# Turning the expert rows on VectorE, from quarters written by ScalarE, in place of TensorE's transposes

## The chip, the cores and the metric

The kernel runs on one core of a Trainium2 chip. The metric is device time in microseconds of one execution, lower is better. TensorE (PE) multiplies and transposes into PSUM, VectorE (DVE) and ScalarE (ACT) do elementwise work, GpSimd (POOL) does some elementwise work and issues the indirect transfers, SyncE (SP) issues the plain ones.

## What is computed

A two-layer backbone over 256 latent tokens and 256 context tokens, width 1024. Each layer has a token mixer and then a mixture of 16 experts of which each token takes two. Layer 0 sends 512 tokens through its experts, layer 1 only the 256 latent ones. The part at stake:

```python
hid = jax.nn.silu(jnp.einsum('bld,edf->blef', h, w_gate)) * jnp.einsum('bld,edf->blef', h, w_up)
y = jnp.einsum('blef,efd->bld', hid * combine[..., None].astype(hid.dtype), w_down)
# D_MODEL = 1024, N_EXPERTS = 16, TOP_K = 2, D_EXPERT = 256, all float32
```

The reference multiplies every token by every expert; `combine` is zero but for the two that the router chose, and the kernel computes those alone.

## The kernel before

**Tiles.** After the router, each expert's tokens are gathered in tiles of 64 slots (`TILE`). With these inputs layer 0 has 24 tiles and layer 1 has 18, some of whose slots are empty. Each engine runs its own loop over the experts and, inside, over the expert's tiles; a tile's number over all experts is `q`.

**One tile, from row to output.** POOL gathers the tile's rows from DRAM into one of two buffers (`rows_in`, line 886): partitions 0 to 63 hold the first half of the width of the 64 slots, partitions 64 to 127 the second half. ACT copies them into `rows_flat` (line 789) in one instruction. PE turns them (`turn`, line 738): 8 transposes of 64x64 into PSUM. DVE copies the result into `slots_T` (line 827), whose eight slices of 64 columns are the stationary operands. PE multiplies gate and up (line 765): 8 slices of the width by 2 halves of the output columns, 16 multiplications, 32 in the trace, since a float32 one leaves two records. ACT takes silu of the gate half (line 800), DVE multiplies it by the up half (line 831), PE turns the product (line 776), DVE copies it out (line 836) and copies the expert's down weights into `down_now` (line 840; in layer 1 it multiplies them by the gate vector, line 843). PE multiplies by them (`down`, line 747), ACT copies the result from PSUM (`y_out`, line 795), and POOL scatters it to DRAM (line 914).

**The order on each engine is written by hand**, as a software pipeline. In its iteration for tile q, PE does gate and up of q, the turn of tile q+1, down of q-1, and the transpose of q's product. ACT does silu of q, the copy of the rows of q+2, and the output of q-1. DVE does the product of q, the copy of the turned rows of q+1, and the two copies for down of q. POOL copies two index columns (lines 903, 906), gathers and then scatters, always in this order, once per iteration; a gather into a buffer waits until ACT has copied the buffer's last rows (`rows_copied`).

**Weights.** SP loads gate, up and down weights of 1 MB each per expert, five experts deep (`sp_gate_up`, `sp_down`). A slot is loaded again when its expert's last gate and up multiplication, and then its last down copy, is done. Each partition k-slice holds rows `(j p k)` of the weights: two runs of 4 KB on a partition.

**Start of a layer.** The first tile's rows are copied, turned and copied out before the first gate and up multiplication can start.

## Time and profile before

| | us |
|---|---|
| Median of 3 runs (897.04 to 899.8) | 898.59 |
| The profiled execution | 899.06 |
| Its span, from first to last instruction | 897.2 |
| PE busy in the span | 762.4 |
| DVE busy | 493.1 |
| ACT busy | 315.3 |
| POOL busy | 308.5 |
| The experts of layer 0, first turn to last output copy | 131.4 to 291.7 |
| The experts of layer 1, the same | 750.6 to 874.7 |

The times of the last two rows are counted from the start of the span. A busy share is an average over stages with different limits; the expert stages are read on their own below. TensorE's clock was granted at 0.917 of full on average, and at full speed through nearly all of both expert stages.

### The profile page before, as it was taken

How to read it: one execution, taken by the hardware profiler on the slowest of the kernel's cores; microseconds unless marked ns; L12 is line 12 of the kernel's file. 1: busy time of each engine (PE TensorE's matmuls, PEld its weight loads, DVE VectorE, ACT ScalarE, POOL GpSimd, SP SyncE). 2: the span in 40 equal slices, each digit the busy share in tenths (PEclk: the TensorE clock that was granted, in tenths of full speed). 3: DMA queues.
4: the chain of work that ended last, by engine and by line, in shares of the span. 5: the costliest groups of instructions: out<-in, count | busy, mean ns of one | idle time of the engine just before them, and what ended most of it. 6: DMA issues, size and time to landing. Idle time of an engine off the chain costs nothing. (4 is left out here: it accounts for less than half of the span.)

```text
span 897.2 us, 15572 instructions
## 1 busy us (share of the span) xinstructions
PE 762.4 (85%) x5261; PEld 439.5 (49%) x5261; DVE 493.1 (55%) x1091; ACT 315.3 (35%) x776; POOL 308.5 (34%) x702
## 2 busy tenths in 40 slices
PE   0988879999999077999999999999988745999986
PEld 0635435555554013655576665766655433555542
DVE  1048754433334593543777677776844653755544
ACT  0250321222222215645557565575641120222220
POOL 0000112343334000275344747447460002445450
PEclk9999869999999569995999999999997955999999
DMA  9999999999891799475351423513110099999933
GB/s 234 397 382 392 418 413 405 408 408 374 316 408 64 283 381 262 160 249 171 90 148 40 121 69 97 154 29 131 43 54 7 13 405 370 402 404 408 406 118 148
DMA packets 107527, 219.34 MB, mean 244 GB/s; under 512 B 28325, under 2 KB 63469, under 8 KB 103105
## 3 DMA queue, kind: packets, MB, share of 16 engines
q1 hardware_dynamic: 98495, 200.39, 62.2%
q0 software_dynamic: 8224, 15.76, 4.6%
q10 hardware_dynamic: 740, 2.32, 0.9%
q8 instruction: 39, 0.64, 0.3%
q14 instruction: 29, 0.24, 0.1%
HBM read 212.09 MB, written 17.33 MB: 256 GB/s over the span
## 5 line engine op out<-in xcount | busy, mean ns | idle before, releaser
L1302 PE MATMUL banks<-h_cols,weight_ring 128*128 128x512 f32 (+1 forms) x384 | 160.7, 539 | 0.7
L1279 POOL TENSOR_TENSOR arena<-arena 128x60 f32<-128x60 f32 (+24 forms) x248 | 82.4, 332 | 125.2 <-DMA arena<-blocks 106.4
L914 POOL DMA_INDIRECT y_of_tokens<-arena,place_now x42 | 60.4, 1437 | 118.7 <-ACT arena L795 105.7
L1281 POOL TENSOR_TENSOR arena<-arena 128x60 f32<-128x60 f32 (+24 forms) x248 | 84.0, 339 | 19.4
L747 PE MATMUL banks<-arena 128*64 128x512 f32 x352 | 85.2, 605 | 4.1 <-DVE arena L843 2.6
L1302 PEld LDWEIGHTS banks<-h_cols,weight_ring 128*128 128x128 f32 x384 | 66.5, 195 | 34.8 <-issue 31.8
L886 POOL DMA_INDIRECT arena<-h_of_tokens,row_now x50 | 52.7, 1055 | 81.9 <-DVE token_of_slot L715 36.7
L287 PE MATMUL banks<-weight_ring,c_cols 128*32 128x512 f32 x368 | 55.2, 721 | 28.0 <-DMA weight_ring<-in_w_mod_dram 28.0
L765 PE MATMUL banks<-weight_ring,arena 128*64 128x256 f32 x576 | 69.1, 394 | 0.9 <-issue 0.9
L800 ACT ACTIVATE arena<-banks 128x128 f32<-128x128 f32 x42 | 11.7, 278 | 145.2 <-PE banks L765 145.2
L831 DVE TENSOR_TENSOR arena<-arena,banks 128x128 f32<-128x128 f32 x42 | 12.1, 288 | 85.2 <-ACT arena L800 62.6
L765 PEld LDWEIGHTS banks<-weight_ring,arena 128*64 128x64 f32 x576 | 41.2, 141 | 22.9 <-issue 3.7
L836 DVE COPY arena<-banks 128x128 f32<-128x128 f32 x42 | 12.3, 292 | 60.0 <-PE banks L776 60.0
L795 ACT COPY arena<-banks 128x512 f32<-128x512 f32 x42 | 24.7, 587 | 52.6 <-PE banks L747 52.6
L789 ACT COPY arena<-arena 128x512 f32<-128x512 f32 x46 | 28.4, 618 | 40.5 <-DMA arena<-h_of_tokens,row_now 27.4
L287 PEld LDWEIGHTS banks<-weight_ring,c_cols 128*32 128x32 f32 x368 | 10.3, 121 | 64.2 <-issue 44.4
L738 PE MATMUL banks<-const,arena 64*128 64x64 f32 x352 | 30.6, 294 | 11.9 <-ACT arena L789 11.9
L1343 DVE SCALAR_TENSOR_TENSOR h_rows<-arena,h_rows 128x512 f32<-128x512 f32 (+1 forms) x64 | 39.5, 618 | 1.6
L738 PEld LDWEIGHTS banks<-const,arena 64*128 64x128 f32 x352 | 24.5, 209 | 29.8 <-issue 20.6
L747 PEld LDWEIGHTS banks<-arena 128*64 128x64 f32 x352 | 21.3, 136 | 32.4 <-issue 25.1
L827 DVE COPY arena<-banks 128x512 f32<-128x512 f32 x44 | 30.4, 692 | 9.9 <-PE banks L738 9.0
L765 PE MATMUL banks<-arena 128*64 128x256 f32 x256 | 31.2, 399 | 1.1 <-DVE arena L827 1.1
(311 smaller groups left out, 1411.7 us busy)
## 6 DMA issues: line engine op xcount, KB each, us to landing
weight_ring<-in_w_mod_dram SPq DMA_DIRECT2D x46, 1024.0 KB, 10.4
weight_ring<-in_dn_w_in_dram SPq DMA_DIRECT2D x32, 512.0 KB, 7.0
weight_ring<-in_w_gate_dram SPq DMA_DIRECT2D x13, 1024.0 KB
weight_ring<-in_w_up_dram SPq DMA_DIRECT2D x13, 1024.0 KB
weight_ring<-in_w_down_dram SPq DMA_DIRECT2D x13, 1024.0 KB
arena<-in_w_gate_dram SPq DMA_DIRECT2D x7, 1024.0 KB
arena<-in_w_up_dram SPq DMA_DIRECT2D x7, 1024.0 KB
arena<-in_w_down_dram SPq DMA_DIRECT2D x7, 1024.0 KB
```

The costliest lines, as they stand in the source:

```text
L287: mm = pe.matmul(m.ps[j * COL:(j + 1) * COL, 0, :], m.c_cols[:, rows * i + k, :], w[:, k, c * BANK:(c + 1) * BANK], start=(i == 0), stop=( ...
L738: mm = pe.transpose(m.ps[:, B_TURN + h, k * TILE:(k + 1) * TILE], v.rows[half, k, :], v.ident[half, half])
L747: mm = pe.matmul(column_half(B_DOWN, h), v.hidden[:, f, :], v.down_now[:, f, h * BANK:(h + 1) * BANK], start=(f == 0), stop=(f == FC - 1))
L765: mm = pe.matmul(column_half(B_GU, h)[:, 0:2 * P], v.slots_T[:, k, :], gate_up(slot, k)[:, :, h * P:(h + 1) * P], start=(k == 0), stop=(k ...
L789: act.copy(v.rows_flat, v.rows_in[u]).then_inc(s(t_ + "rows_copied"), 1)
L827: dve.tensor_copy(v.slots_T.rearrange("p (h k) n -> p h (k n)", h=2), turned_rows).then_inc(s(t_ + "slots_T"), 1)
L886: pool.indirect_dma_start(v.rows_in[u], None, h_halves, bass.IndirectOffsetOnAxis(m.row_now[:, at:at + 1], 0), bounds_check=last_half, oob ...
L914: pool.indirect_dma_start(y_halves, bass.IndirectOffsetOnAxis(m.place_now[:, u:u + 1], 0), v.y_tile[u], None, bounds_check=last_row, oob_i ...
L1279: then(pool.tensor_tensor(part, U[:, 0:q, j:j + 1].to_broadcast([P, q, BLK - 1 - j]), M[:, j, j + 1:BLK].unsqueeze(1).to_broadcast([P, q, ...
L1281: ins = pool.tensor_tensor(U[:, 0:q, j + 1:BLK], U[:, 0:q, j + 1:BLK], part, ALU.subtract)
L1302: mm = pe.matmul(bank(6 + j % 2)[:, 0:CTX + SEQ - n0], head_w[h % 2][:, j, k, :], m.hT[:, k, n0:CTX + SEQ], start=(k == 0), stop=(k == KD ...
L1343: ins = dve.scalar_tensor_tensor(out=out, in0=src, scalar=tap, in1=out, op0=ALU.mult, op1=ALU.add)
```

## The change

It takes the turning of the rows from PE and gives it to DVE.

- ACT copies a tile's rows from `rows_in` into `rows_flat` in eight instructions of 32 partitions by 256 elements, four for the first 32 slots and four for the other 32 (`copied(u, a)`). Partition group q of `rows_flat` then holds quarter q of the width. The output copy `y_out` stands between the two fours.
- DVE turns each half tile with one 32x32-block transpose of 128 partitions by 256 elements, straight into `slots_T` (`turned(a)`), twice a tile. It reads every eighth element. The first stands ahead of the product of q, the second behind it.
- PE's `turn` and DVE's copy from PSUM are gone, and the wait of the gate and up multiplication on `rows_copied`.
- The weights' rows are laid on partitions as `(p k)` in place of `(j p k)`: one run of 8 KB on a partition, where the slot is whole. The slot in pieces (slot 4, 3 of 16 experts a layer) keeps runs of 4 KB, and so do the down weights.
- The gather is still one transfer a tile, and waits for the second four of ACT's copies.

```diff
-    v.rows = v.rows_flat.rearrange("p (n k) -> p k n", k=KD // 2)
+    v.rows = v.rows_flat.rearrange("p (a n k) -> p a k n", a=2, k=KD)
...
-                    sp.dma_start(whole[slot][:, a, :].rearrange("p (j n) -> p j n", j=2),
-                                 w.rearrange("(j p k) f -> p j (k f)", j=2, p=P)).then_inc(done, 16)
+                    sp.dma_start(whole[slot][:, a, :], w.rearrange("(p k) f -> p (k f)", p=P)).then_inc(done, 16)
...
-                    pe.wait_ge(s(t_ + "slots_T"), q + 1)
+                    pe.wait_ge(s(t_ + "slots_T"), 2 * q + 2)
                     for k in range(KD):
-                        if k == KD - 1:
-                            pe.wait_ge(s(t_ + "rows_copied"), q + 2)
...
-                    turn().then_inc(s(t_ + "turned"), 1)
...
-            def copied(u):
-                act.copy(v.rows_flat, v.rows_in[u]).then_inc(s(t_ + "rows_copied"), 1)
+            def copied(u, a):
+                for q in range(4):
+                    slots, col = TILE * (q // 2) + SUB * a, QUARTER * (q % 2)
+                    ins = act.copy(v.rows_flat[q * SUB:(q + 1) * SUB, a * QUARTER:(a + 1) * QUARTER],
+                                   v.rows_in[u][slots:slots + SUB, col:col + QUARTER])
+                ins.then_inc(s(t_ + ("rows_copied" if a else "rows_first")), 1)
...
-                act.wait_ge(s(t_ + "turned"), q + 1)
+                act.wait_ge(s(t_ + "slots_T"), 2 * q + 3)
                 act.wait_ge(s(t_ + f"rows{u}"), 16 * j + 32)
-                copied(u)
+                copied(u, 0)
                 put_out()
+                act.wait_ge(s(t_ + "slots_T"), 2 * q + 4)
+                copied(u, 1)
...
-            def turned():
-                dve.tensor_copy(v.slots_T.rearrange("p (h k) n -> p h (k n)", h=2), turned_rows).then_inc(s(t_ + "slots_T"), 1)
+            def turned(a):
+                dve.transpose(v.slots_T[:, :, a * SUB:(a + 1) * SUB], v.rows[:, a, :, :]).then_inc(s(t_ + "slots_T"), 1)
 
             def tile(e, q):
+                dve.wait_ge(s(t_ + "gate_up"), q + 1)
+                dve.wait_ge(s(t_ + "rows_first"), q + 2)
+                turned(0)
                 dve.wait_ge(s(t_ + "silu"), q + 1)
                 dve.tensor_tensor(v.hid_rows, v.silu, m.ps[:, B_GU, P:2 * P], ALU.mult).then_inc(s(t_ + "hid_rows"), 1)
-                dve.wait_ge(s(t_ + "turned"), q + 1)
-                turned()
+                dve.wait_ge(s(t_ + "rows_copied"), q + 2)
+                turned(1)
```

On PE, one pass of the loop of an expert of layer 0, before. L765 is gate and up, L738 the turn, L747 down, L776 the product's transpose; L483 and L484 load the next expert's tile counts.

```order
L760 ISA
L765 MATMUL banks<-weight_ring,arena 64x256 x14
L763 REGISTER_ALU
L765 MATMUL banks<-weight_ring,arena 64x256 x2
L483 TENSOR_LOAD tile_counts
L483 ISA x2
L484 TENSOR_LOAD tile_counts
L484 ISA x2
L738 MATMUL banks<-const,arena 128x64 x8
L747 MATMUL banks<-arena 64x512 x4
L776 MATMUL banks<-const,arena 128x128
```

The same pass on PE in the changed kernel, where these are L754, L740 and L763.

```order
L751 ISA
L754 MATMUL banks<-weight_ring,arena 64x256 x16
L484 TENSOR_LOAD tile_counts
L484 ISA x2
L485 TENSOR_LOAD tile_counts
L485 ISA x2
L759 REGISTER_ALU
L740 MATMUL banks<-arena 64x512 x4
L763 MATMUL banks<-const,arena 128x128
```

The eight transposes have gone from between gate and up and down, and the loads of the counts now stand directly ahead of down.

On ACT, one tile of its loop before: silu (L800), the copy of the rows (L789), the output (L795).

```order
L800 ACTIVATE arena<-banks 128x128
L802 ISA
L789 COPY arena<-arena 128x512
L792 ISA
L794 REGISTER_ALU
L795 COPY arena<-banks 128x512
```

The same tile on ACT in the changed kernel: silu is L791, the copies of the rows L778, the output L786.

```order
L791 ACTIVATE arena<-banks 128x128
L792 ISA
L793 ISA
L778 COPY arena<-arena 32x256 x4
L783 ISA
L785 REGISTER_ALU
L786 COPY arena<-banks 128x512
L796 REGISTER_ALU
L778 COPY arena<-arena 32x256 x4
```

One copy has become four ahead of the output and four behind it.

## Rows read from the trace of the kernel before

**Rows 1.** Chain that ended last, layer 1: start, length in us, what.

```profile
841.43 0.62 PE banks L738 x8
842.06 1.87 PE banks L747 x8
843.92 0.26 PE banks L776
844.18 3.60 PE banks L765 x32
```

**Rows 2.** Timeline of PE, layer 0: turns of the first and last tiles.

```profile
138.68 0.69 PE L738 MATMUL banks<-const,arena 64*128 64x64 f32 x8
...
284.81 0.69 PE L738 MATMUL banks<-const,arena 64*128 64x64 f32 x8
```

**Rows 3.** Timeline of ACT and DVE in a mixer: four small operations in a row.

```profile
674.08 1.64 ACT L1603 COPY arena<-arena 32x256 f32<-32x256 f32 x4 [6.80 <-DMA arena<-inverted_blocks]
...
674.08 1.78 DVE L1562 STREAM_TRANSPOSE arena<-arena 32x256 f32<-32x256 f32 x4 [0.18 <-DMA arena<-inverted_blocks]
```

**Rows 4.** Timeline, one tile of layer 1, all engines; in brackets the idle time before.

```profile
797.01 0.28 ACT L800 ACTIVATE arena<-banks 128x128 f32<-128x128 f32 x1 [3.20 <-PE banks L765]
...
797.63 0.69 DVE L827 COPY arena<-banks 128x512 f32<-128x512 f32 x1
...
799.58 0.59 ACT L795 COPY arena<-banks 128x512 f32<-128x512 f32 x1 [1.25 <-PE banks L747]
...
799.96 2.28 DVE L843 TENSOR_TENSOR arena<-weight_ring,modulation 128x2048 f32<-128x2048 f32 x1
...
800.97 2.16 POOL L914 DMA_INDIRECT y_of_tokens<-arena,place_now  x1 [2.98 <-ACT arena L795]
...
804.22 1.03 POOL L886 DMA_INDIRECT arena<-h_of_tokens,row_now  x1 [0.77 <-POOL row_now L906]
```

**Rows 5.** Timeline of ACT: copies of the rows that waited for their gather.

```profile
248.39 0.62 ACT L789 COPY arena<-arena 128x512 f32<-128x512 f32 x1 [1.30 <-DMA arena<-h_of_tokens,row_now]
...
810.42 0.62 ACT L789 COPY arena<-arena 128x512 f32<-128x512 f32 x1 [0.42 <-PE banks L738]
...
823.99 0.62 ACT L789 COPY arena<-arena 128x512 f32<-128x512 f32 x1 [1.29 <-DMA arena<-h_of_tokens,row_now]
```

**Rows 6.** Timeline of POOL: gathers (L886) and, before one, its scatter.

```profile
238.05 1.10 POOL L914 DMA_INDIRECT y_of_tokens<-arena,place_now  x1 [3.13 <-ACT arena L795]
240.25 1.04 POOL L886 DMA_INDIRECT arena<-h_of_tokens,row_now  x1 [0.77 <-POOL row_now L906]
...
816.92 1.03 POOL L886 DMA_INDIRECT arena<-h_of_tokens,row_now  x1 [0.77 <-POOL row_now L906]
```

**Rows 7.** A stretch of layer 1: busy PE, PEld, DVE, ACT, POOL, PEclk, DMA share, GB/s.

```profile
852.00:858.00 6.00, 6.00 (x49) 3.15 (x47) 3.11 (x5) 1.48 (x3) 3.29 (x4) 1.00 0.81 324
```

**Rows 8.** SP's queue in 762:850, then in 312:328: packets, MB, share.

```profile
q1 hardware_dynamic: 8541, 32.52, 92.9%
...
q1 hardware_dynamic: 946, 6.81, 101.5%
```

**Rows 9.** Timeline of POOL: the last store of h in layer 0, in layer 1.

```profile
101.20 0.53 POOL L878 DMA_DIRECT2D h_of_tokens<-h_rows  x1 [0.66 <-DVE h_rows L372]
...
724.45 0.55 POOL L878 DMA_DIRECT2D h_of_tokens<-h_rows  x1 [0.56 <-DVE h_rows L372]
```

**Rows 10.** Timeline of SP: the first load that waited for those stores, in each layer.

```profile
117.29 0.37 SPq L460 DMA_DIRECT2D h_rows<-in_w_gate_dram  x1
...
734.50 0.37 SPq L460 DMA_DIRECT2D h_rows<-in_w_gate_dram  x1
```

**Rows 11.** Chain, start of layer 1's experts.

```profile
749.89 0.63 ACT arena L789
...
752.21 6.63 PE banks L765 x32
```

**Rows 12.** Timeline of PE, the first gate and up of layer 0.

```profile
133.23 5.52 PE L765 MATMUL banks<-arena 128*64 128x256 f32 x32 [1.10 <-DVE arena L827]
```

More of the change, by code:

```diff
@@ L42 @@
 TILES = 36
+SUB = TILE // 2
+QUARTER = D // 4
 PAD = 8 * MT * P
@@ L459, in sp_gate_up @@
                 if slot < EXPERT_SLOTS - 1:
-                    sp.dma_start(whole[slot][:, a, :].rearrange("p (j n) -> p j n", j=2),
-                                 w.rearrange("(j p k) f -> p j (k f)", j=2, p=P)).then_inc(done, 16)
+                    sp.dma_start(whole[slot][:, a, :], w.rearrange("(p k) f -> p (k f)", p=P)).then_inc(done, 16)
                 else:
                     for j in range(2):
-                        sp.dma_start(pieces[j][:, a, :, :], w.rearrange("(j p k) f -> j p k f", j=2, p=P)[j]).then_inc(done, 16)
+                        sp.dma_start(pieces[j][:, a, :, :], w.rearrange("(p j k) f -> j p k f", j=2, p=P)[j]).then_inc(done, 16)
         def sp_down(sp, L, e):
@@ L723, in build @@
         h_halves = h_dram.rearrange("r (h n) -> (r h) n", h=2)
-        B_GU, B_HID, B_TURN, B_DOWN = 0, 2, 5, 7
-        turned_rows = m.ps[:, B_TURN:B_TURN + 2, 0:KD // 2 * TILE]
+        B_GU, B_HID, B_DOWN = 0, 2, 7
         def pe_moe(pe, L):
             t_ = L.tag
-            def turn():
-                for k in range(KD // 2):
-                    for h in range(2):
-                        half = slice(h * TILE, (h + 1) * TILE)
-                        mm = pe.transpose(m.ps[:, B_TURN + h, k * TILE:(k + 1) * TILE], v.rows[half, k, :], v.ident[half, half])
-                return mm
             def column_half(bank, h):
@@ L749, in down @@
                 mm.then_inc(s(t_ + "down"), 1)
-            pe.wait_ge(s(t_ + "rows_copied"), 1)
-            turn().then_inc(s("turned_first"), 1)
             pe.wait_ge(s("router_meta"), L.n + 1)
@@ L800, in tile @@
                 act.activation(v.silu, m.ps[:, B_GU, 0:P], ACT.Silu).then_inc(s(t_ + "silu"), 1)
-                act.wait_ge(s(t_ + "turned"), q + 1)
+                act.wait_ge(s(t_ + "slots_T"), 2 * q + 3)
                 act.wait_ge(s(t_ + f"rows{u}"), 16 * j + 32)
-                copied(u)
+                copied(u, 0)
                 put_out()
+                act.wait_ge(s(t_ + "slots_T"), 2 * q + 4)
+                copied(u, 1)
             act.sem_inc(s(t_ + "y_tile"), 2)
             act.wait_ge(s(t_ + "rows0"), 16)
-            copied(0)
-            act.wait_ge(s("turned_first"), L.n + 1)
+            for a in range(2):
+                copied(0, a)
             act.wait_ge(s(t_ + "rows1"), 16)
-            copied(1)
+            for a in range(2):
+                act.wait_ge(s(t_ + "slots_T"), a + 1)
+                copied(1, a)
             act.wait_ge(s("router_meta"), L.n + 1)
@@ L852, in dve_moe @@
                 dve.sem_inc(s(t_ + "hidden"), 1)
-            dve.wait_ge(s("turned_first"), L.n + 1)
-            turned()
+            for a in range(2):
+                dve.wait_ge(s(t_ + ("rows_copied" if a else "rows_first")), 1)
+                turned(a)
+            dve.wait_ge(s("router_meta"), L.n + 1)
             nt, tb = expert_count(dve, 0)
```

## Prediction

> **What bounds the kernel now.** I read the expert stages first, since the change touches nothing else. The chain of waits through layer 1 is PE alone: of one tile, 0.62 us of turn, 1.87 of down, 0.26 of transpose, 3.60 of gate and up, 6.35 in all and without a gap [rows 1]. In layer 0 the turns of the second and the last tile but one lie 146.13 us and 23 tiles apart, again 6.35 each [rows 2]. So PE sets the pace of all 42 tiles, and what the reader must ask is who is next in line. Three candidates: the two engines that take over the work, the gather of the rows, whose round trip hangs on ACT and POOL [rows 4 to 6], and the stream of weights [rows 7, 8]. After the experts of layer 0 PE is idle until about 312, so what that stage saves moves everything behind it.
>
> **The turn on PE.** It goes 42 times at 0.62 us [rows 1]: **-26.0 us**, if PE keeps its pace, then 5.73 us a tile. The loads of the tile counts that stand between gate and up and the turn now stand ahead of down; today they make no gap there [rows 1], so I cost them at nothing. PE next needs the down weights' copy: today DVE ends it at 802.24 and down starts at 803.87 (gate and up ends at 803.24, then the turn). In the new tile down starts 0.62 earlier after gate and up, but DVE's chain starts earlier by the same 0.62, so some 1.0 us of cover stays.
>
> **ACT.** No row has the new copies, the nearest are its 32x256 copies in a mixer, four in 1.64 us [rows 3]. Per tile ACT has silu 0.28, four copies 1.64, output 0.59 and four copies 1.64, 4.15 us of 5.73. Counted from the end of gate and up: the first four start at about 0.5 (silu, and DVE's first transpose), end at 2.15, the output (down ends at 1.87) at 2.8, the second four at 4.4. ACT fits, at no cost, as long as the rows have landed. Even at 0.62, the price of today's copy of 512 elements on 128 partitions [rows 5], eight would be 4.96 and ACT 5.83, 0.1 us a tile or 4 in all.
>
> **DVE.** Two transposes in place of one copy of 0.69 [rows 4]. Nearest row: 32x256, four in 1.78, so 0.44 each [rows 3]; 128 partitions are four such blocks side by side. The new ones read with a step of eight elements, which no row has; I bound them by 0.44 and 0.69, the row with twice the elements, and take 0.44. In layer 1 DVE then has about 3.8 us of 5.73, and both transposes end by 1.3 us into the tile, where gate and up wants them at 2.13: no cost, at 0.69 either (1.8). A page of the Trainium skill, SBUF - State Buffer (section Door 1), says that reads which leave a 16-byte line at each element pay a penalty, and these do. No run here shows that yet; at double the time, 0.88, the second would end at 2.1, still level with PE's need, and each layer would start 0.44 later.
>
> **The start of a layer.** In front of the first gate and up stand now: two fours of copies, 3.28, the second transpose, 0.44, and some 0.25 of hand-overs, 3.9 us, against 2.32 today (749.89 to 752.21) [rows 11]. That is +1.6 in layer 1, +1.5 in layer 0. The first gate and up runs partly at PE's half clock, 6.63 and 5.52 us for what is 3.60 at full [rows 11, 12]; with PE idle for longer ahead of it the rise comes later, between 0 and 0.6 in layer 1 (7.2 is all of it at half) and 0 and 1.7 in layer 0. I take 1.0 for both. **+4.1 us** (3.1 to 5.4).
>
> **The gather.** This is the new danger. From the end of one output copy: 0.80 us to the scatter's start (800.17 to 800.97) [rows 4], 2.20 from there to the next gather's start (240.25 - 238.05) [rows 6], L until the rows land, the first four copies 1.64, the output 0.59. By then two tiles have passed, so a tile lasts at least (5.23 + L)/2; today it is (4.2 + L)/2. L shows only where ACT waited: 823.99 - 816.92 = 7.07 [rows 5, 6], 248.39 - 240.25 = 8.14, and elsewhere it is below, as in 810.42 - 804.22 = 6.2 [rows 4, 5]. ACT's waits of this kind number 8 in layer 1 beyond the first and four in layer 0 (two of them in rows 5); with each one's gather they put L between 6.1 and 7.3 in layer 1, and at 7.3 to 8.1 in those four of layer 0. Below L = 6.23 PE paces; my middle is 6.4 to 6.6, a loop of 5.8 to 5.9. ACT can slip some 2.3 us before PE feels it (silu must start by 1.1 into the tile, so the output may end at 5.2 and not 2.8), and only the 16 tiles of layer 0 and 17 of layer 1 that run under a full weight stream have such an L. (0.18 x 16) - 2.3 = **+0.6 us** in layer 0, and in layer 1 nothing beyond the next term. In layer 1 the scatter takes 2.16 us in place of 1.10, since it ends 0.9 after DVE's L843 [rows 4]; that eats 0.9 of the slip, and gives it back when ACT is late.
>
> **The weights.** In layer 1 the stream is full until 852 + 6 x 0.81/1.03 = 856.7 [rows 7], and PE starts the last expert at 863.24, only 6.5 later. The new PE would want it at 863.24 - 17 x 0.62 + 2.1 = 854.8. The first slot comes free about 2.1 later, so the stream would end at 858.8 and PE wait 4.0 us. But runs of 8 KB move faster: with w_mod's, 6.81 MB in 946 packets, SP's queue moved 426 GB/s at 101.5% share, 419 at full; with 4 KB, 32.52 MB in 8541 packets, 370 at 92.9%, 398 at full [rows 8]. 2.1 MB of an expert then take 5.0 and not 5.3 us; 13 whole experts, 3.5. The stream ends at 855.3: **+0.5 us**, with 4.0 if the packets bring nothing. Layer 0 has 1.5 tiles an expert, so its stream has some 10 us of cover at the end and keeps 1 to 3.
>
> **Sum.** 899.06 - 26.0 + 4.1 + 0.6 + 0.5 = 878.3. The profiled execution is 0.5 above the median of the runs; I say 878.5 for the median.
>
> **Rivals.** *The gather paces (889).* If L is 7.2 wherever the stream is full, the loop is 6.2 us, 0.48 over PE's: 16 x 0.48 - 2.3 and 17 x 0.48 - 1.4 give 12.2 in place of 1.1, so 889. For it: L reaches 7 to 8 in rows of both layers. Against it: most copies in layer 0 found their rows there 7.2 after the gather's start, and half of those in layer 1 at 6.2.
>
> *Slower, by the gather (913).* The same loop decides the sign: above L = 7.5 it is over 6.35, and the kernel loses. Its way there is competition: the weights' packets double to 8 KB, and a gather's packets of 2 KB queue between them. With L at 8.14 all through, a tile lasts 6.69: 41 x 0.96 - 3.5 = 35.9 lost, 899 - 26 + 4 + 36 = 913. Against it: POOL's four stores of h (2.1 MB) were done 16.1 us after the last was issued under w_mod's 8 KB packets (101.2 to 117.3), its two (1.05 MB) 10.0 us after under 4 KB ones (724.5 to 734.5), 130 and 105 GB/s [rows 9, 10]: no slower beside the larger packets. The Trainium skill, DMA: Bandwidth & Descriptors (section Queues, rings and completion order), says that a DMA engine goes round the queues packet by packet, a packet holding many descriptors. By that rule it is the bytes of a whole packet, not of one run, that the gather waits for, and these stay the same. The stores' rates agree with it.
>
> *The weights pace layer 1 (882).* The 8 KB runs bring nothing: +3.5. This lies in the forecast's own range.
>
> *The change doesn't free PE (899).* PE's gap stays, by the counts' loads or by a late product, and the turns' time is idle: 0.62 a tile. Rows 1 show no gap there and the product is ready 1.8 us before PE wants it.
>
> **Chances.** Forecast, 874.5 to 885: 0.66. Gather-paced, 885 to 896: 0.2. Within 0.3% (2.7 us, about what a measurement of this kernel can tell): 0.05. Slower: 0.09. Faster is 0.86. The low end is 26.0 less 3.1 alone, 876, and 1.5 for faster loads in layer 0's start or elsewhere; the high end goes into the gather's case, 891.
>
> **What would show it.** PE's groups of gate and up, down and transpose follow without gaps at 5.73 us. ACT's 32x256 copies take 0.41 and L786 ends 2.8 after gate and up; if the gather paces, ACT's copies have waits on the gather in most tiles and PE waits for DVE's product or ACT's output. DVE's transposes take 0.44; 0.9 would mean that the step costs. The experts of layer 0 last some 13 us less, of layer 1 some 8 less. PE waits for weights only at the last expert. The forecast is wrong if L moved, or if a copy of 32 partitions costs more here than in the mixer.

## The result: 0.5% faster, not 2.2%

The changed kernel takes 892.36 us (median of 10 runs, 888.17 to 896.28) against 896.98 for the kernel before in the same sessions (10 runs, 895.38 to 899.8). The ratio is 0.995 with a 95% interval of 0.9936 to 0.9964: 4.6 us faster, where 20 were forecast. The profiled execution took 889.70 us, 2.7 below that median, with a span of 887.9, and the profiled one of before had a span of 897.2. That one of before lies 2.1 above its median of 896.98. The stages below are compared in these two spans, whose difference is 9.3, and not 4.6.

The page of the changed kernel, busy time first (the part on the chain gives shares of the span by engine, then by line; the groups give count, busy and mean ns, idle before and its releaser):

```profile
span 887.9 us, 15344 instructions
...
PE 728.6 (82%) x4909; PEld 417.1 (47%) x4909; DVE 512.1 (58%) x1135; ACT 433.9 (49%) x1098; POOL 305.3 (34%) x702
...
PE 8%; DMA 7%; DVE 3%; ACT 2%; issue 2%; SPq 2%; DVEq 0%; POOL 0%; POOLq 0%; ACTq 0%
...
L778 ACT COPY arena<-arena 32x256 f32<-32x256 f32 x368 | 148.1, 402 | 91.9 <-DMA arena<-h_of_tokens,row_now 82.3
...
L822 DVE STREAM_TRANSPOSE arena<-arena 128x256 f32<-128x256 f32 x88 | 56.2, 639 | 96.6 <-PE banks L754 71.2
```

PE is busy for 34 us less (762.4 before), and the span is only 9 us shorter: most of what PE was relieved of has become idle time of PE. The group of ACT's new copies says behind what: 82 us of idle time ahead of them end with the gather, 17.3 of it ahead of layer 1's first copy.

The chain through layer 1 says the same. Before it was PE alone [rows 1]. Now, in 760:850 of the span (line shares of the chain, then start, length, what):

```profile
by line: DMA arena<-h_of_tokens,row_now 33.4%; DMA weight_ring<-in_w_down_dram 24.1%; issue 10.5%; ACT arena L778 9.2%; SPq L476 5.5%; SPq L465 5.3%; PE banks L754 4.1%; SPq L462 2.5%; DVE arena L841 2.4%; PE banks L740 1.9%; DVE arena L822
...
756.86 8.29 DMA arena<-h_of_tokens,row_now
765.23 0.40 ACT arena L778
765.64 0.40 ACT arena L778
766.06 0.40 ACT arena L778
766.47 0.40 ACT arena L778
766.90 0.59 ACT arena L786
```

A gather, four copies, the output: that is the loop which the prediction called the new danger. Its way from one gather to the next but one is not always the output and its scatter: from 767.51 the chain goes on through the second four copies to POOL, and the next gather on it starts at 770.40, 5.2 us after the landing, as long as the way that the prediction had priced at 5.23. The chain holds a second thing, a quarter of the stretch:

```profile
831.67 21.66 DMA weight_ring<-in_w_down_dram
```

That is the last load of weights, to the last expert's gate and up at 853.47. So the end of layer 1 hangs on the stream of weights too; on the chain that load was issued after a slot that DVE's down step freed at 816.19, and the gathers stand ahead of that.

ACT's waits for the gather, first in the stretch of layer 0's experts, then in layer 1's behind the first tile (total us, times, longest):

```profile
ACT arena L778 <- DMA arena<-h_of_tokens,row_now: 35.1, 17, 4.0
...
ACT arena L778 <- DMA arena<-h_of_tokens,row_now: 29.9, 13, 4.3
```

and the same two of the kernel before:

```profile
ACT arena L789 <- DMA arena<-h_of_tokens,row_now: 3.7, 4, 1.3
...
ACT arena L789 <- DMA arena<-h_of_tokens,row_now: 6.6, 8, 1.5
```

Here is one late gather of layer 0 and what it does to the engines; it was issued at 158.37 and the copies start 7.17 us later (timeline; in brackets the idle time before and its releaser):

```profile
158.37 1.04 POOL L886 DMA_INDIRECT arena<-h_of_tokens,row_now  x1 [0.77 <-POOL row_now L906]
...
165.54 1.65 ACT L778 COPY arena<-arena 32x256 f32<-32x256 f32 x4 [2.90 <-DMA arena<-h_of_tokens,row_now]
167.21 0.58 ACT L786 COPY arena<-banks 128x512 f32<-128x512 f32 x1
167.82 1.65 ACT L778 COPY arena<-arena 32x256 f32<-32x256 f32 x4
...
167.94 1.94 PE L740 MATMUL banks<-arena 128*64 128x512 f32 x8
...
169.49 0.28 ACT L791 ACTIVATE arena<-banks 128x128 f32<-128x128 f32 x1
...
169.79 0.29 DVE L829 TENSOR_TENSOR arena<-arena,banks 128x128 f32<-128x128 f32 x1 [1.12 <-issue]
170.00 0.63 DVE L822 STREAM_TRANSPOSE arena<-arena 128x256 f32<-128x256 f32 x1
...
170.14 0.33 PE L763 MATMUL banks<-const,arena 128*128 128x128 f32 x1 [0.27 <-DVE arena L829]
...
170.69 0.65 PE L754 MATMUL banks<-modulation,arena 128*64 128x256 f32 x4 [0.22 <-DVE arena L822]
```

The late rows hold four copies, the output and four more copies on ACT, then the next silu stands behind all nine, then DVE's product behind silu, then PE's transpose and gate and up. ACT is not the bound by its busy time (49% of the span), but it carries the delay of the gather to PE.

Stage by stage, in the two spans (us):

| | before | after | difference |
|---|---|---|---|
| start to the first silu of layer 0 | 138.80 | 140.05 | +1.3 |
| first to last silu of layer 0, 23 tiles | 146.13 | 140.07 | -6.1 |
| from there to the landing of layer 1's first rows | 465.0 | 461.8 | -3.2 |
| landing to the first silu of layer 1 | 9.0 | 9.7 | +0.7 |
| first to last silu of layer 1, 17 tiles | 108.00 | 105.87 | -2.1 |
| last silu to the end | 30.3 | 30.4 | +0.1 |

The third row has no change in it. In the kernels measured here it lies between 461.8 and 465.2, so most of its -3.2 can be the scatter of single executions. The first row scatters as much: in the changed kernel and its variants the first silu starts between 137.7 and 140.7, so the +1.3 is not resolved either.

### The profile page after: what moved, and what is told of

The parts are those of the page before. It is cut to its first block and busy times, and to the rows that moved or that the text cites. A ratio compares the mean times of both kernels' runs of the same rounds, so it can differ in the third digit from the quotient of the medians.

```text
span 887.9 us, 15344 instructions
## 1 busy us (share of the span) xinstructions
PE 728.6 (82%) x4909; PEld 417.1 (47%) x4909; DVE 512.1 (58%) x1135; ACT 433.9 (49%) x1098; POOL 305.3 (34%) x702
## 3 DMA queue, kind: packets, MB, share of 16 engines
q10 hardware_dynamic: 740, 2.32, 0.9%
## 5 line engine op out<-in xcount | busy, mean ns | idle before, releaser
L778 ACT COPY arena<-arena 32x256 f32<-32x256 f32 x368 | 148.1, 402 | 91.9 <-DMA arena<-h_of_tokens,row_now 82.3
L822 DVE STREAM_TRANSPOSE arena<-arena 128x256 f32<-128x256 f32 x88 | 56.2, 639 | 96.6 <-PE banks L754 71.2
L886 POOL DMA_INDIRECT arena<-h_of_tokens,row_now x50 | 64.2, 1284 | 91.4 <-DVE token_of_slot L716 36.6
L740 PE MATMUL banks<-arena 128*64 128x512 f32 x352 | 84.7, 601 | 11.3 <-ACT arena L786 6.8
L754 PE MATMUL banks<-weight_ring,arena 128*64 128x256 f32 x576 | 68.1, 390 | 16.1 <-DVE arena L822 14.0
L914 POOL DMA_INDIRECT y_of_tokens<-arena,place_now x42 | 45.1, 1073 | 99.0 <-ACT arena L786 94.0
L754 PEld LDWEIGHTS banks<-weight_ring,arena 128*64 128x64 f32 x576 | 41.1, 140 | 37.8 <-DVE arena L822 15.8
L740 PEld LDWEIGHTS banks<-arena 128*64 128x64 f32 x352 | 25.4, 137 | 45.5 <-issue 37.0
L754 PE MATMUL banks<-arena 128*64 128x256 f32 x256 | 31.9, 406 | 6.8 <-DVE arena L822 6.7
L1741 ACT ACTIVATE arena<-banks,arena 128x128 f32<-128x128 f32 x24 | 8.7, 364 | 49.8 <-PE banks L1685 49.8
L1785 PE MATMUL banks<-weight_ring,modulation 128*128 128x512 f32 x64 | 30.9, 634 | 0.6 <-ACT modulation L1773 0.6
L1311 PE MATMUL banks<-weight_ring,h_cols 128*128 128x128 f32 x256 | 30.7, 278 | 0.1
L1311 PEld LDWEIGHTS banks<-weight_ring,h_cols 128*128 128x128 f32 x256 | 29.2, 192 | 2.6 <-ACT arena L1320 1.8
L309 DVE TENSOR_TENSOR mod_sums<-banks,mod_sums 128x512 f32<-128x512 f32 x8 | 5.5, 684 | 42.3 <-PE banks L289 42.3
```

The costliest lines, as they stand in the source:

```text
L740: mm = pe.matmul(column_half(B_DOWN, h), v.hidden[:, f, :], v.down_now[:, f, h * BANK:(h + 1) * BANK], start=(f == 0), stop=(f == FC - 1))
L754: mm = pe.matmul(column_half(B_GU, h)[:, 0:2 * P], v.slots_T[:, k, :], gate_up(slot, k)[:, :, h * P:(h + 1) * P], start=(k == 0), stop=(k ...
L778: ins = act.copy(v.rows_flat[q * SUB:(q + 1) * SUB, a * QUARTER:(a + 1) * QUARTER], v.rows_in[u][slots:slots + SUB, col:col + QUARTER])
L822: dve.transpose(v.slots_T[:, :, a * SUB:(a + 1) * SUB], v.rows[:, a, :, :]).then_inc(s(t_ + "slots_T"), 1)
L886: pool.indirect_dma_start(v.rows_in[u], None, h_halves, bass.IndirectOffsetOnAxis(m.row_now[:, at:at + 1], 0), bounds_check=last_half, oob ...
L914: pool.indirect_dma_start(y_halves, bass.IndirectOffsetOnAxis(m.place_now[:, u:u + 1], 0), v.y_tile[u], None, bounds_check=last_row, oob_i ...
```

## The experiments

The theory after the result: **the gather's loop paces the tiles**, because L, the time from a gather's start on POOL to the start of the copies that wait for it, is 7.1 us and not the 6.4 to 6.6 assumed, and because four copies stand in the loop ahead of the output. Rivals: ACT's number of copies by itself; the 8 KB runs of the weights; the bytes of the gather; DVE's down step, which holds up POOL's issue of a gather; the transposes' stride.

### PE's turn shortened in the kernel before

```diff
-                for k in range(KD // 2):
-                    for h in range(2):
-                        half = slice(h * TILE, (h + 1) * TILE)
-                        mm = pe.transpose(m.ps[:, B_TURN + h, k * TILE:(k + 1) * TILE], v.rows[half, k, :], v.ident[half, half])
+                for h in range(2):
+                    half = slice(h * TILE, (h + 1) * TILE)
+                    mm = pe.transpose(m.ps[:, B_TURN + h, 0:TILE], v.rows[half, 0, :], v.ident[half, half])
```

> The kernel before, with PE's turn cut from eight transposes to two; everything else, the copies, the waits and DVE's copy from PSUM too, stays. The rows are then not turned, so the experts' outputs are of stale columns. Theory G (a gather's round trip through ACT and POOL paces the changed kernel, because ACT's four copies of 1.64 us stand between the gather and the output): here only 0.62 us stand there, so the loop is (4.2 + L)/2, 5.65 us a tile at L = 7.1; PE's tile is 6.35 - 0.47 = 5.88. So the full gain of PE's time: 42 x 0.47 = 20 us less, about 878, few long waits of PE. Rival W (the pace is the weights' stream or something on PE that the turn covers, and freeing PE brings nothing with any copy): within 3 us of before in layer 0 and no more than 5 in all. Rival L (L itself grows when PE runs faster, since gathers, scatters and weights crowd): L rises beyond 8 and about half of the gain is lost, 888.

Measured: 887.59 us (885.12 to 888.76), ratio 0.9881 (0.9859 to 0.9902). In layer 0 every tile lasts 5.99 us in place of 6.35 and the 23 tiles 137.85, so with one copy of the rows on ACT each 0.36 us taken from PE is gained whole. In layer 1 the 17 tiles take 106.91, only 1.1 less. One wait eats the rest (timeline of PE):

```profile
843.51 3.42 PE L764 MATMUL banks<-modulation,arena 128*64 128x256 f32 x16 [3.06 <-DMA mod_sums<-in_w_down_dram]
846.76 1.90 PE L764 MATMUL banks<-h_cols,arena 128*64 128x256 f32 x16
```

PE waits 3.06 us for the last expert's weights, and behind the wait the first 16 multiplications take 3.42 and the second 1.90: TensorE's granted clock had fallen, to 0.58 of full between 844 and 847. The theory had forecast 878, with all of PE's time gained in both layers. The 888 forecast for a longer L was met in number alone: L is not longer here. What follows: PE's share of the argument holds, and the stream of weights is the next limit in layer 1. A kernel with 0.36 us less on PE, and nothing added elsewhere, already beats the changed one.

### The eight copies put into the kernel before

```diff
-            def copied(u):
-                act.copy(v.rows_flat, v.rows_in[u]).then_inc(s(t_ + "rows_copied"), 1)
+            def copied(u, a):
+                for q in range(4):
+                    part, cols = slice(32 * q, 32 * q + 32), slice(256 * a, 256 * a + 256)
+                    ins = act.copy(v.rows_flat[part, cols], v.rows_in[u][part, cols])
+                if a:
+                    ins.then_inc(s(t_ + "rows_copied"), 1)
...
-                copied(u)
+                copied(u, 0)
                 put_out()
+                copied(u, 1)
```

> The kernel before, with ACT's one copy of the rows replaced by eight of 32 x 256, four ahead of the output and four behind it, same data, same place; PE's turn stays. Theory G: a tile's loop is (5.23 + L)/2, 6.2 at L = 7.1, just under PE's 6.35, so the time moves little: 897 to 901, with the first tiles of both layers 2.7 us later each and some PE stalls where L exceeds 7.5. If ACT's eight copies alone cost more than I think (rival A: ACT is the engine that paces), 905 or more. If they cost nothing but the start: 900 to 902.

Measured: 906.66 us (902.13 to 908.69), ratio 1.0098 (1.0059 to 1.0138), 9.1 slower. The 23 tiles of layer 0 take 147.36 (+1.2), the 17 of layer 1 109.81 (+1.8), and the two starts are 1.6 and 2.0 later, 6.6 in all, of a span that is 6.0 longer in the profiled execution. The theory had 897 to 901 for the time. The median lies in the range, 905 or more, that the expectation had given to ACT as the engine that paces. The periods speak against it: at PE's old pace of 6.35 the loop with the copies in it almost fits, and 29 of the 40 periods stay at 6.35 or 6.36; the others reach 7.06. What rules it out is the run with most of the weights left out, further down: there ACT does all its eight copies in tiles of 5.58 us. The copies are not ACT's limit by their number; they are a part of the loop.

### The weights' runs, undone and done alone

In the changed kernel, back to 4 KB runs (the same rows on the same partitions, gate and up interleaved by halves):

```diff
-                return whole[slot].rearrange("p a (k f) -> p a k f", k=KD)[:, :, k, :]
+                return halves(slot)[:, k // (KD // 2)].rearrange("p a (k f) -> p a k f", k=KD // 2)[:, :, k % (KD // 2), :]
...
-                    sp.dma_start(whole[slot][:, a, :], w.rearrange("(p k) f -> p (k f)", p=P)).then_inc(done, 16)
+                    sp.dma_start(halves(slot)[:, :, a, :], w.rearrange("(p j k) f -> p j (k f)", j=2, p=P)).then_inc(done, 16)
```

> The changed kernel with its weights in runs of 4 KB again, of the same rows on the same partitions (gate and up interleaved by halves in the slot). Rival C (the 8 KB runs lengthen the gather, since its packets queue behind larger ones): L falls from about 7.1 to 6.4 and the time by 6 to 12 us, to 881 to 886. Theory G with L as it always was (my 6.4 to 6.6 was read too low out of rows that only bound it): L stays at 7.0 to 7.2, the time stays or rises by up to 4 us, since the stream of layer 1 is 3.5 us slower: 892 to 896.

And the kernel before with 8 KB runs:

```diff
-                    sp.dma_start(whole[slot][:, a, :].rearrange("p (j n) -> p j n", j=2),
-                                 w.rearrange("(j p k) f -> p j (k f)", j=2, p=P)).then_inc(done, 16)
+                    sp.dma_start(whole[slot][:, a, :], w.rearrange("(p k) f -> p (k f)", p=P)).then_inc(done, 16)
```

> The kernel before with its weights in runs of 8 KB, on other rows' partitions than the tokens' columns, so the experts multiply by the wrong rows. Does only the change of the loads. PE paces at 6.35 us there, so the time is the same, 896 to 899. What is looked for is the stream: in layer 1 it should end some 3.5 us sooner than at 856.7 if larger runs move faster, and ACT's waits for gathers should grow, by 0.3 to 0.4 us a gather, if larger runs hold gathers up.

Measured: with 4 KB runs 892.34 us (891.22 to 893.94), ratio 0.9939 (0.992 to 0.9957), the same time as with 8 KB. The kernel before with 8 KB runs took 897.74 (895.43 to 899.95, 10 runs), ratio 1.0006 (0.9992 to 1.0021): no change. Inside, two small effects cancel. SP's queue in 760:845, first of the changed kernel, then with 4 KB runs (packets, MB, share):

```profile
q1 hardware_dynamic: 6271, 31.30, 90.9%
```

```profile
q1 hardware_dynamic: 8069, 30.72, 90.5%
```

At full share that is 405 and 399 GB/s, 1.4% and not the 5% that [rows 8] had promised. The gather, on the other side, lands sooner beside 4 KB runs: over the copies that waited, L averages 6.71 in layer 0 (19 of them) and 6.59 in layer 1 (13), against 7.08 (17) and 7.18 (13) in the changed kernel. In the kernel before, 8 KB runs moved ACT's waits in layer 1 from 8 to 12 and the mean L from 6.81 to 7.02. With 4 KB runs layer 0 is 3.6 us shorter (136.48), and layer 1 3.3 us longer (109.15), since there PE waits for weights at four places, up to 3.2 us, as in the first experiment. So the two effects cancel in the changed kernel's time, and not because there was nothing to gain.

Means over the copies that waited are a choice of the long gathers, and a different one in each kernel. The trace also tells of the others: each transfer leaves up to 16 signals on its semaphore, and the last of them is its landing. The time from a gather's start to the last signal recorded, averaged over the gathers in whose first 6 us SP's queue held over 80% of the engines (us; in brackets how many gathers):

| | weights in runs of 4 KB | weights in runs of 8 KB |
|---|---|---|
| kernel before, layer 0 | 6.57 (18) | 6.90 (15) |
| kernel before, layer 1 | 6.48 (15) | 6.74 (16) |
| changed kernel, layer 0 | 6.48 (17) | 6.92 (17) |
| changed kernel, layer 1 | 6.38 (16) | 7.07 (14) |

A waiting copy starts some 0.08 us behind that signal. Where some of the 16 are missing from the trace the reading is a little short; with the complete gathers alone the eight means are 6.4 to 6.6 and 6.7 to 7.3. In the two other kernels with 4 KB runs the means of a layer are 6.3 to 6.5, and in the four others that keep the changed kernel's weights and gathers 6.5 to 7.2. So the 8 KB runs lengthen the gathers under the stream by some 0.3 to 0.7 us, which is 0.15 to 0.35 us of a tile's loop (over both layers together the difference is 0.28 in the kernel before, with a standard error of 0.14, and 0.56 in the changed one, with 0.16). Without them the changed kernel gains 3.6 us in layer 0. The rival is right in kind: its L of 6.4 came, and its 881 to 886 did not, because layer 1 gave the gain back to the weights.

### A gather that moves nearly nothing

```diff
-            last_half = pool.to_reg(2 * MT * P - 1)
+            first_rows = pool.to_reg(1)
...
-                                        bounds_check=last_half, oob_is_err=False).then_inc(s(t_ + f"rows{u}"), 16)
+                                        bounds_check=first_rows, oob_is_err=False).then_inc(s(t_ + f"rows{u}"), 16)
```

> The changed kernel with a bound on its gathers that lets only the first two half rows through, so nearly no row is moved, and the tiles compute on zeros; every instruction and wait stays. Theory G: L falls to about 3 us, the loop to 4.1, and PE paces at 5.6 to 5.7 us a tile in both layers but for the weights: 874 to 880, PE hardly waits between the first and the last tile. Rival W (weights or PE's own issue): it stays at 889 to 893 and PE waits as before. Rival A (ACT's 4.15 us a tile pace together with their waits on DVE): tiles of 6 us or more stay.

Measured: 882.12 us (879.08 to 885.95), ratio 0.9818 (0.9783 to 0.9853). The expectation was an L of 3 and 874 to 880. The surprise is how little L shrinks where ACT waited: 6.65 on average in layer 0 (15 waits, 5.85 to 7.56), 6.95 in layer 1 (12). ACT still waits, 26.9 us in layer 0:

```profile
ACT arena L778 <- DMA arena<-h_of_tokens,row_now: 26.9, 15, 3.5
```

By the landing signals the mean is 6.42 in layer 0 and 6.80 in layer 1, where the changed kernel has 6.92 and 7.07. So most of L is not the time to move 256 KB of rows, but latency of an indirect transfer that is issued while SP's queue holds some 90% of the engines. It does not follow that a smaller gather buys nothing: the median is 10.2 us below the changed kernel's, more than the new order on ACT brings below. An L shorter by 0.50 and 0.27 us would be 8 us over the 40 tiles, an estimate from the signals. But these tiles compute on zeros, and the two of the four executions that took 879 us had a mean granted clock of 0.923 and 0.927 where the changed kernel's ten have 0.912 to 0.922. How the 10 us divide stays open. The Trainium skill, DMA: Bandwidth & Descriptors (section Anatomy of one DMA), fits a transfer from this path by some 2.0 us and the bytes at 436 GB/s, for 256 KB an estimate of 2.6; in the changed kernel and in this one L is never below 5.78 among the copies that waited in the tiles, so under a full stream the measurement decides.

### Most of the weights not loaded

From the sixth expert of a layer on, an eighth of gate and up and half of down are loaded (two of the edited lines):

```diff
+                    run = 8 * 2 * P if e < EXPERT_SLOTS else 2 * P
+                    sp.dma_start(whole[slot][:, a, 0:run], w.rearrange("(p k) f -> p (k f)", p=P)[:, 0:run]).then_inc(done, 16)
...
+            cols = D if e < EXPERT_SLOTS else 2 * P
```

> The changed kernel with only the first five experts' weights of a layer loaded in full; of every later expert an eighth of gate and up and half of down is loaded, so its output is of stale weights. All instructions and waits stay, the stream of weights is mostly gone. Theory G: L is long because the gather waits behind the stream; without it L falls to 4 to 5 us (4.7 is what the first gather of layer 1 shows, from a queue with 3 MB before it), the loop to 5.0, and PE paces at 5.58 a tile once the first five experts are in: 868 to 876, ACT's waits for gathers under 5 us a layer beyond the first. Rival A (ACT and DVE in series pace at 6 us): 885 or more.

Measured: 870.02 us (868.39 to 870.98), ratio 0.9691 (0.9664 to 0.9718). By the landing signals the gathers that are issued with SP's queue at under half of the engines land after 3.4 us on average (30 of them, both layers), against 6.9 to 7.1 in the changed kernel: the stream makes L. (The 4.7 us of the expectation is counted from the second gather of layer 1, as 745.18 to 749.89 in the kernel before; the first copy waits for the first gather, issued at 743.07, 6.8 us ahead.) With the stream gone the loop is gone: in layer 1 no copy waits for its gather behind the first, and the 17 tiles take 94.85 us, 5.58 each. A stretch of it, then the same one of the changed kernel (busy PE, PEld, DVE, ACT, POOL, PEclk, DMA share, GB/s):

```profile
800.00:830.00 30.00, 30.00 (x218) 15.32 (x216) 20.93 (x31) 22.00 (x55) 15.20 (x21) 1.00 0.39 118
```

```profile
800.00:830.00 30.00, 24.92 (x182) 12.71 (x180) 17.32 (x22) 19.17 (x47) 12.29 (x17) 1.00 1.02 412
```

PE is busy without a gap while ACT does all its eight copies a tile and is busy for 22 us of 30, DVE for 21. ACT and DVE therefore fit beside PE, as the prediction said. The tile of PE by itself, layer 0:

```profile
248.39 3.67 PE L757 MATMUL banks<-weight_ring,arena 128*64 128x256 f32 x32
251.90 1.89 PE L743 MATMUL banks<-arena 128*64 128x512 f32 x8
253.71 0.33 PE L766 MATMUL banks<-const,arena 128*128 128x128 f32 x1
253.97 3.67 PE L757 MATMUL banks<-weight_ring,arena 128*64 128x256 f32 x32
```

253.97 - 248.39 = 5.58: the turn was worth 0.77 us a tile and not 0.62. The changed kernel shows it too, at the end of layer 0, when its stream has ended.

### DVE's down step in pieces

The down step is cut in pieces, each with its own operation. The suspicion was that a long one holds up POOL's issue of a gather, as here in the changed kernel, layer 1:

```profile
794.12 2.28 DVE L841 TENSOR_TENSOR arena<-weight_ring,modulation 128x2048 f32<-128x2048 f32 x1
794.16 3.14 POOL L886 DMA_INDIRECT arena<-h_of_tokens,row_now  x1 [0.77 <-POOL row_now L906]
```

```diff
-                        ins = dve.tensor_copy(to, of)
+                    step = BANK if L.n == 0 else D
+                    for c in range(0, to.shape[1], step):
...
+                            ins = dve.tensor_copy(to[:, c:c + step], of[:, c:c + step])
...
+                            ins = dve.tensor_tensor(to[:, c:c + step], of[:, c:c + step], mod_vec(GATE2), ALU.mult)
```

> The changed kernel with DVE's down-weight step in pieces: in layer 0 four copies of 512 elements for one of 2048, in layer 1 two products of 1024 for one of 2048. Theory P (POOL issues the gather late, held up for as long as a DVE instruction on two ports runs; that is part of why L is longer than before): the gathers of over 1.3 us, 12 in layer 0 and 3 in layer 1 of the changed kernel, go to 1.04 to 1.2, ACT's waits for gathers shrink by a fifth to a third, the time to 886 to 890. If POOL is held by something else, gathers of 1.4 to 3.1 us stay, and 892 to 894.

Measured: 892.68 us (889.06 to 896.86, 10 runs), ratio 0.9955 (0.9936 to 0.9975), the time of the changed kernel. The long issues did vanish (in the stretches of the tiles 15 gathers took over 1.3 us in the changed kernel, and one does here), and with them some of L, in layer 0 from 7.08 to 6.57 on average, in layer 1 only from 7.18 to 7.06. Yet ACT's waits are still 34.3 us at 17 places in layer 0, which takes 138.71 us, 1.4 less, and layer 1's 17 tiles take 105.63, 0.2 less. POOL's issue is a small part of L, and as the cause of the pace this theory falls. One thing stays open: by the signals L is 6.51 in layer 0, as short as with 4 KB runs, and yet layer 0 is 2.2 us longer than there. L alone doesn't set the pace to the last microsecond.

### The transposes without the stride

```diff
-    v.rows = v.rows_flat.rearrange("p (a n k) -> p a k n", a=2, k=KD)
+    v.rows = v.rows_flat.rearrange("p (a k n) -> p a k n", a=2, k=KD)
```

> The changed kernel whose DVE transposes read 256 neighbouring elements in place of every eighth, so the columns come in the wrong order. If the step costs, an instruction takes 0.44 us as the small ones in the mixer do and not 0.64; if it is the 128 partitions that cost, it stays at 0.64. The time moves by less than 3 us either way, since DVE's transposes end before PE wants them, but where ACT is late they stand in its way, 0.2 us each.

Measured: 893.5 us in one run, not to be told from the changed kernel. Its group of transposes:

```profile
L822 DVE STREAM_TRANSPOSE arena<-arena 128x256 f32<-128x256 f32 x88 | 38.7, 440 | 94.7 <-PE banks L754 67.9
```

440 ns in place of 639: reading every eighth element costs 0.2 us an instruction, 1.45 times the plain one. It costs the kernel nothing that one run could show.

### ACT's output ahead of the copies

```diff
+                put_out()
                 act.wait_ge(s(t_ + "slots_T"), 2 * q + 3)
                 act.wait_ge(s(t_ + f"rows{u}"), 16 * j + 32)
                 copied(u, 0)
-                put_out()
```

> The changed kernel with ACT's output copy moved ahead of the first four copies of the rows. The gather then no longer stands in front of the output and so of POOL's next scatter and gather: the round trip is copies (3.28), POOL's index column and 0.77 us, and L, some 11.3 us at L = 7.0 and so 5.65 a tile, with ACT at 5.8 (it waits for down before its first copy). Theory G: the pace in both layers falls to 5.8 to 5.9 us, the time to 882 to 886, and POOL waits for the output less. Rival P (the waits are from gathers that POOL issues late, under DVE's copy of the down weights, whatever ACT's order): 888 to 892, and gathers of 1.4 to 3.1 us remain. If ACT, now with its waits in series, paces: 6.1 us a tile, 890 or more.

Measured: 887.48 us (885.54 to 890.86), ratio 0.9902 (0.9869 to 0.9935). The forecast was 882 to 886. This is the version that beats both kernels, the changed one by 4.9 us in the medians; its interval and the changed kernel's, 0.9936 to 0.9964, just miss each other. The 23 tiles of layer 0 take 133.04 in place of 140.07, and there ACT waits for gathers 9.7 us in place of 35.1. A late gather now holds the eight copies, but not the output that has to leave before the next gather is issued. What the next gather waits for is the end of the copies (timeline, ACT and then POOL, layer 1):

```profile
789.60 3.31 ACT L778 COPY arena<-arena 32x256 f32<-32x256 f32 x8
...
794.03 1.03 POOL L886 DMA_INDIRECT arena<-h_of_tokens,row_now  x1 [0.77 <-POOL row_now L906]
```

From the copies' end at 792.91 to the gather's start are 1.12 us, then L, then 3.31 of copies: the loop is (4.4 + L)/2, near the (4.2 + L)/2 of the kernel before, in place of (5.23 + L)/2. The tiles of layer 0 last 5.78. L itself is hardly shorter: 7.37 on average where ACT waited in layer 0, and 6.84 by the signals of all. In layer 1 the 17 tiles take 105.43, hardly less than 105.87, and the rows say why (timeline of PE; then two stretches of the windows):

```profile
829.10 0.33 PE L763 MATMUL banks<-const,arena 128*128 128x128 f32 x1
832.41 6.58 PE L754 MATMUL banks<-h_rows,arena 128*64 128x256 f32 x32 [2.99 <-DMA h_cols<-in_w_down_dram]
```

```profile
826.00:832.00 6.00, 3.42 (x23) 1.46 (x19) 3.85 (x5) 4.27 (x12) 3.07 (x5) 0.96 1.02 408
832.00:838.00 6.00, 5.59 (x26) 3.15 (x28) 0.00 (x0) 1.18 (x3) 2.26 (x4) 0.50 1.03 407
```

PE has outrun the stream: it waits 2.99 us for the weights of an expert, and the gate and up behind it runs at a granted clock of 0.50 and takes 6.58 in place of 3.67. One wait of 3 us costs 6.

### Both together

The same order on ACT, and the down step in pieces as well; the edits are the two above.

> Both edits, the output ahead of the rows' copies and DVE's down step in pieces: the candidate. Theories G and P: layer 0 closer to PE's own 5.58 us a tile (24 tiles in 130 to 132 us from the first silu to the last, against 133.1 with the output first alone and 140.0 in the changed kernel); layer 1 stays bound by the weights' stream at its end, about 105 us from first silu to last. 884 to 886.

Measured: 890.01 us (885.49 to 893.45, 6 runs), ratio 0.9925 (0.9897 to 0.9953), and not the 884 to 886 forecast. Its interval overlaps that of the new order alone; pieces add nothing here either. Layer 0 takes 132.48, layer 1 107.40.

## Why the prediction was wrong

**The step that failed is the gather's term, +0.6 us: the L in it, and the slip taken off it.** The prediction named the right loop, (5.23 + L)/2, and took L as 6.4 to 6.6 where the stream is full. In the changed kernel L is 7.08 in layer 0 and 7.18 in layer 1 over the copies that waited, 6.92 and 7.07 by the landing signals of all. With 7.1 the loop is 6.17 us a tile; the silus lie 140.07 / 23 = 6.09 and 105.87 / 17 = 6.23 apart. The prediction's own rival *the gather paces*, worked out for L = 7.2, said 889, and the profiled execution took 889.7 (the median is 892.36).

The middle of 6.4 to 6.6 was no misreading of the kernel before: by the signals its gathers land after 6.57 and 6.48 us. What failed is the assumption that L would stay as it was. The change itself lengthened it, mainly by its 8 KB runs, as the table above shows; the prediction had this competition among its rivals and set it aside. Its first reason, the stores' rates, is of four and of two plain stores, and tells nothing of an indirect gather's latency. Its second was that the bytes of a packet stay the same when the runs grow; this was the prediction's own step from the rule that it cited, and no run shows it. The gathers beside 8 KB runs landed later, which refutes its conclusion.

The few waits of the kernel before would not have been the better reading. Their mean in layer 0 was 7.75 us, from four copies of 23, the latest ones, and would have made a loop of 6.49 and a slower kernel. Waits alone read too long, as bounds without a wait say only that L was no longer.

**The slip was mis-sized too.** The 2.3 us by which ACT may be late were subtracted once a stretch. But a late gather is passed to PE by nine instructions of ACT in a row, as shown at 165.54, and in layer 0 periods of 4.9 to 5.6 and of 6.4 to 8.2 us follow one another: variation of L costs, and its slack isn't saved up. The variant with 4 KB runs shows the size. There L is 6.4 to 6.5, as forecast, and layer 0 takes 136.48 us where the forecast had 132.4. So of the 7.7 us by which the changed kernel's layer 0 is longer than forecast some 4 are the slip and some 3.6 the longer L, as far as one execution of each can tell.

**A second round trip was left out.** POOL copies the next tile's index only when the scatter of two tiles before has landed. In the kernel before its L903 never waited for that in these stretches; in the changed one it does, here for layer 0 (total, times, longest):

```profile
POOL place_now L903 <- DMA y_of_tokens<-arena,place_now: 5.4, 6, 2.0
```

In the kernel with the output first it is 9.5 us at 10 places, so a part of what remains above 5.58 there may be the scatter's. No run here took that wait away, so how much time it is worth stays open.

**The turn.** Right in kind, and too small: 5.58 us of PE a tile in place of 6.35, 0.77 and not 0.62, in the stretches where nothing else paces.

**Two of the 42 turns brought nothing.** PE turned 44 times and not 42: besides the first of each layer, which stands in the start's term, there is one behind the last gate and up of each, for a tile that doesn't come. In layer 1 the last down started 0.78 us sooner after the last gate and up (8.23 in place of 9.01 behind its start), and took 2.85 us in place of 1.94, at a granted clock of 0.66 (1.00 before); so the stage's end is no shorter. Timeline of PE, before and after:

```profile
863.17 3.67 PE L765 MATMUL banks<-weight_ring,arena 128*64 128x256 f32 x32
...
872.18 1.94 PE L747 MATMUL banks<-arena 128*64 128x512 f32 x8 [2.58 <-DVE arena L843]
```

```profile
861.70 2.85 PE L740 MATMUL banks<-arena 128*64 128x512 f32 x8 [2.58 <-DVE arena L841]
```

**The start of a layer** was +4.1 and is +2.0 in these two executions, of which layer 0's +1.3 lies in the scatter. In layer 1 the first gate and up starts 4.03 us after the rows landed against 2.32, +1.7 where +1.6 was forecast. The clock's part went the other way: that gate and up took 5.65 us, not 6.63 [rows 11], and in layer 0 6.21, not 5.52 [rows 12], -1.0 and +0.7 where +1.0 stood for both. The first rows, landing and multiplication, of layer 1 after:

```profile
741.88 6.64 ACT L778 COPY arena<-arena 32x256 f32<-32x256 f32 x16 [17.30 <-DMA arena<-h_of_tokens,row_now]
...
745.91 5.65 PE L754 MATMUL banks<-weight_ring,arena 128*64 128x256 f32 x32 [12.62 <-DVE arena L822]
```

**ACT and DVE.** Both fit by their busy time; what costs is where ACT's copies stand in the loop. ACT's copies take 0.40 us as forecast, DVE's transposes 0.64, near the bound of 0.69 and not the 0.44 taken. The rule of the Trainium skill that was weighed (SBUF - State Buffer, section Door 1) has the direction, a penalty for reads with a step beyond a 16-byte line; the plain read is 0.44 and the strided one 0.64. The double was the prediction's own assumption and is too much.

**The weights.** The place was right: in layer 1 PE waits for them once, for the last expert.

```profile
853.47 3.67 PE L754 MATMUL banks<-weight_ring,arena 128*64 128x256 f32 x32 [1.98 <-DMA weight_ring<-in_w_down_dram]
```

The reason was not: 8 KB runs brought 1.4% and not 5%, and the wait was 2 us with a PE that came late itself. In the two kernels whose PE came sooner, with the output first and with PE's turn shortened, it is 3.0 and 3.1 us, and the lower clock behind it costs more: as much again with the output first.

**The sum with what was measured.** It is 878.3, and 7.7 for layer 0 (140.07 in place of 23 x 5.73 + 0.6), 8.0 for layer 1 (105.87 in place of 17 x 5.73 + 0.5), -2.1 for the starts, +0.7 for the end of layer 1 (+0.1 in place of a turn less), and -2.6 for the stretch between the layers (-3.2 in place of a turn less): 890.0 against 889.70. The stages are taken from that execution, so this closes by itself; it says where the time lies and proves no cause.

## What to carry to other kernels

When an engine is relieved, the next limit is often a round trip and not a busy engine: write down each loop that runs through a transfer, with every instruction that stands in it, and put the one that feeds the transfer first on its engine. A transfer's latency read only where somebody waited comes out too long, since the late ones are those that are waited for, and rows without a wait only bound it; the landing signals of all transfers give the mean. Then ask whether the change itself moves it, here by larger runs in the queue beside it. Don't take slack off a varying wait once for a whole stretch. And see what the freed engine runs into: here a wait of 3 us for weights also took TensorE's clock, and cost 6.

## What was not expected of the hardware

- An indirect gather of 64 slots, issued while SP's queue held 91% of the engines (368 GB/s in 760:845), took 6.1 to 8.8 us from its start to the first reader, where that one waited. With almost no bytes moved it took 5.8 to 8.6, and with the stream mostly gone it landed after 3.4 on average.
- SP's queue moves 399 GB/s at full share in runs of 4 KB and 405 in runs of 8 KB, and the larger runs lengthen the gathers beside them: landing means of 6.4 to 6.6 us became 6.7 to 7.1.
- TensorE's granted clock was 0.50 in the 6 us behind a wait of 2.99 us, and 0.96 in the 6 us that held the wait. Gate and up took 6.58 us there.
- A gather issued 0.04 us behind the start of a 2.28 us VectorE multiplication was busy on POOL for 3.14 us instead of 1.03. That long issue did not set the pace.
- A 32x32-block transpose of 128x256 float32 takes 440 ns reading in order and 639 ns with a step of eight elements.
